# A reordered hand-written schedule around attention: the copies of values, the window sums, and the reload of the residual

## The reference

```python
h = _rmsnorm(x, norm1) @ w_in              # -> c_q (256), c_kv (128), k_rope (32), u (512)
q = einsum('bsr,rhd->bshd', _rmsnorm(c_q, q_a_norm), w_q_b)
kv = einsum('bsr,rhd->bshd', _rmsnorm(c_kv, kv_a_norm), w_kv_b)   # 8 heads, k_nope and v
attn = softmax((q_nope . k_nope + rope(q_rope) . rope(k_rope)) * scale) @ v
pool = einsum('bsgc,gcd->bsgd', window_mean(u) - u, pool_w) * pool_scale  # windows 2, 4, 8, 16
x = x + concat([attn, pool]) @ w_out
up = dwconv3(_rmsnorm(x, norm2) @ w_up); x = x + (silu(gate) * val) @ w_down
x = x + (p @ w_ple_proj) * sigmoid(_rmsnorm(x, norm3) @ w_ple_gate + b_ple_gate)
y = _rmsnorm(x, final_norm)
```

## Time and profile before

| | |
|---|---|
| median of 3 runs | 1244.72 us (1244.24 to 1246.07) |
| the profiled execution | 1244.72 us, span 1242.7 us |
| mean granted TensorE clock | 0.994 |
| TensorE busy | 1204.8 us |
| VectorE, ScalarE, GpSimd busy | 708.8, 462.7, 204.5 us |

### The profile page before, as it was taken

The page is one execution under the profiler, slowest core; times in us unless marked ns, Lnnn a source line. Parts: engine busy times, 40 slices in busy tenths (PEclk is TensorE's granted clock), DMA queues, the critical chain, the costliest instruction groups (busy, mean ns, idle before and its releaser), DMA issues.

```text
span 1242.7 us, 15574 instructions
## 1 busy us (share of the span) xinstructions
PE 1204.8 (97%) x5496; PEld 970.4 (78%) x5496; DVE 708.8 (57%) x979; ACT 462.7 (37%) x744; POOL 204.5 (16%) x216
## 2 busy tenths in 40 slices
PE   6999799999999999999999999999999999999996
PEld 5887666666888888888888888888788888888885
DVE  6648876763577565554555555555433465347665
ACT  5411577774233433323232322323223344325333
POOL 0137532323654000000000000000000021002100
PEclk9999899999999999999999999999999999999999
DMA  5510000104342222232212222221444444443341
GB/s 191 205 43 11 11 12 11 35 18 159 95 119 85 65 90 66 68 102 68 84 61 75 67 68 84 68 84 61 141 135 143 152 143 140 148 126 95 102 145 76
DMA packets 119187, 113.46 MB, mean 91 GB/s; under 512 B 6292, under 2 KB 102891, under 8 KB 118379
## 3 DMA queue, kind: packets, MB, share of 16 engines
q1 hardware_dynamic: 118848, 112.84, 28.8%
q10 hardware_dynamic: 298, 0.11, 0.0%
HBM read 93.01 MB, written 19.92 MB: 91 GB/s over the span
## 4 chain that ended last, share of the span: by engine, by line
PE 90%; DVE 5%; ACT 3%; issue 1%; DMA 1%; POOL 0%; DVEq 0%; SPq 0%; ACTq 0%
PE ps L194 28%; PE ps L196 28%; PE ps L195 28%; PE ps L575 2%; PE ps L556 2%; ACT SF L917 1%; PE ps L450 1%; PE ps L567 1%; DVE WDHL L1330 1%; PE ps L443 1%; DVE TL L1601 1%; DMA WR<-in_w_ple_gate 1%; DVE XL L1191 0%; PE ps L428 0%; DVE XT L1190 0%
## 5 line engine op out<-in xcount | busy, mean ns | idle before, releaser
L194 PE MATMUL ps<-XH,WH 128*128 128x512 f32 x1096 | 434.2, 396 | 8.6 <-DVE XL L1412 5.1
L195 PE MATMUL ps<-XL,WH 128*128 128x512 f32 x1096 | 428.0, 391 | 0.0
L196 PE MATMUL ps<-XH,WL 128*128 128x512 f32 x1096 | 428.0, 390 | 0.0
L229 DVE TENSOR_TENSOR WL<-WR,WH 128x1024 fp32r<-128x1024 f32 (+1 forms) x133 | 175.7, 1321 | 186.9 <-ACT WH L224 186.6
L224 ACT ACTIVATE WH<-WR 128x1024 fp32r<-128x1024 f32 (+1 forms) x133 | 138.1, 1039 | 320.9 <-PE ps L196 310.8
L194 PEld LDWEIGHTS ps<-XH,WH 128*128 128x128 f32 x1096 | 206.4, 188 | 55.4 <-issue 8.8
L195 PEld LDWEIGHTS ps<-XL,WH 128*128 128x128 f32 x1096 | 206.6, 189 | 44.1 <-issue 2.4
L196 PEld LDWEIGHTS ps<-XH,WL 128*128 128x128 f32 x1096 | 206.6, 189 | 43.3
L1063 ACT ACTIVATE SF<-SF,col 128x512 f32<-128x512 f32 x88 | 71.7, 816 | 289.0 <-DVE SF L1475 288.9
L1475 DVE TENSOR_TENSOR SF<-ps,R 128x512 f32<-128x512 f32 x88 | 60.5, 688 | 169.1 <-PE ps L196 163.7
L194 PE MATMUL ps<-GHL,WH 128*128 128x512 f32 x352 | 137.1, 389 | 0.8 <-DVE SF L1475 0.8
(11 more groups left out here) (164 smaller groups left out, 1244.5 us busy)
## 6 DMA issues: line engine op xcount, KB each, us to landing
WR<-in_w_up SPq DMA_DIRECT2D x44, 512.0 KB, 3.8
WR<-in_w_down SPq DMA_DIRECT2D x44, 512.0 KB, 3.6
g_scratch<-SF SPq DMA_DIRECT2D x22, 512.0 KB, 2.8
SF<-g_scratch SPq DMA_DIRECT2D x44, 256.0 KB, 3.7
WR<-in_w_out SPq DMA_DIRECT2D x16, 512.0 KB, 3.7
WR<-in_w_ple_gate SPq DMA_DIRECT2D x16, 512.0 KB, 3.7
WR<-in_w_in SPq DMA_DIRECT2D x8, 512.0 KB, 5.1
xt_scratch<-XT SPq DMA_DIRECT2D x2, 2048.0 KB, 13.0
```

The costliest lines, as they stand in the source:

```text
L194: pe.matmul(out, wh, xh, start=first, stop=False)
L195: pe.matmul(out, wh, xl, start=False, stop=False)
L196: return pe.matmul(out, wl, xh, start=False, stop=last)
L229: dve.tensor_tensor(WL[:, slot(n), base:cols, :], WR[:, slot(n), base:cols, :], WH[:, slot(n), base:cols, :].bitcast(F32), ALU.subtract).t ...
```

## The change

Nothing of the computation differs; only places and waits do.

- SP: the four reload quarters wait once, for `o_lo` 8 (the last output of attention split), instead of `o_ready` 7 for the first two and `o_ready` 8 for the others.
- TensorE: `values(i + 1, 0)` goes from u 8 to u 12 and waits for the row sums of pair i, sequence 0 to be copied; `weigh(i, 0)` no longer waits for the copy of `values(i + 1, 0)`. `project_q(i + 1, 1)` goes from u 11 to u 9.
- ScalarE: in each slot the exponent is ahead of the turned copy; `q_split(i + 1, 1)` from u 13 to 11, the copy of the values from u 9 to 13.
- VectorE: `rotate(i + 1, 1)` from u 12 to 10, `q_low(i + 1, 1)` from 14 to 12. At input tile 7 the window sums of group 1 come behind the splits of the first attention weights instead of ahead of them.

```diff
--- before.py
+++ after.py
@@ -315,9 +315,8 @@
                     for n in range(T_OUT, T_OUT + 4):
                         sp.wait_ge(w_lo, n - 1)
                         sp.dma_start(WR[:, slot(n), :, :], wtile(w["w_out"][:, (n - T_OUT) * P:(n - T_OUT + 1) * P])).then_inc(ring_in[slot(n)], 16)
+                    sp.wait_ge(o_lo, HEADS)
                     for q in range(4):
-                        if q % 2 == 0:
-                            sp.wait_ge(o_ready, HEADS - 1 + q // 2)
                         sp.dma_start(XT[:, q * 2048:(q + 1) * 2048], xt_dram[:, q * 2048:(q + 1) * 2048]).then_inc(xt_back[q], 16)
                 with sp.Fori(0 if s else 2, KT // 2) as i:
                     for c in range(2):
@@ -520,8 +519,8 @@
                 bank = 7 if i else 4 + s
                 if i and s:
                     pe.wait_ge(v_copied, i * 2 + 1)
-                elif i >= 2:
-                    pe.wait_ge(rr_copied, i * 2 - 2)
+                elif i:
+                    pe.wait_ge(rr_copied, i * 2 - 1)
                 for t in range(TT):
                     tok = slice(t * P, (t + 1) * P)
                     o = ps[bank][:, t * P:(t + 1) * P]
@@ -562,7 +561,7 @@
                     pe.wait_ge(dr_ready, i * 2 + s + 1)
                     if i or s:
                         pe.wait_ge(rr_copied, i * 2 + s)
-                    pe.wait_ge(v_copied, i * 2 + s + 1 + (i < HEADS // 2 - 1) * 2)
+                    pe.wait_ge(v_copied, i * 2 + s + 1 + (s and i < HEADS // 2 - 1) * 2)
                     for h in range(2):
                         ins = pe.matmul(ps[7][h * V_DIM:(h + 1) * V_DIM, :], ones[:, 0:V_DIM], DR[h], start=True, stop=True)
                     ins.then_inc(rr_ready, 1)
@@ -614,10 +613,10 @@
                             project_q(i + 1, 0, qf_ready, i * 4 + 4)
                         if u == 7:
                             project_k(i + 1, 0, qf_ready, i * 4 + 5)
-                        if u == 8:
+                        if u == 9:
+                            project_q(i + 1, 1, k_lo, i * 4 + 6)
+                        if u == 12:
                             values(i + 1, 0)
-                        if u == 11:
-                            project_q(i + 1, 1, k_lo, i * 4 + 6)
                         if u == 13:
                             project_q(i + 1, 2, qf_ready, i * 4 + 6)
                         if u == 15:
@@ -938,11 +937,11 @@
 
             def pair(i, last):
                 for u in range(4 * TT):
-                    turned(i, u)
                     if u + 2 < 4 * TT:
                         exponent(i, u + 2)
                     elif not last:
                         exponent(i + 1, u + 2 - 4 * TT)
+                    turned(i, u)
                     if i:
                         if u == 0:
                             k_split(i, 1)
@@ -976,10 +975,10 @@
                             q_split(i + 1, 0)
                         if u == 8:
                             k_split(i + 1, 0)
-                        if u == 9:
+                        if u == 11:
+                            q_split(i + 1, 1)
+                        if u == 13:
                             values(i + 1, 0)
-                        if u == 13:
-                            q_split(i + 1, 1)
                         if u == 15:
                             q_split(i + 1, 2)
                 if last:
@@ -1263,9 +1262,9 @@
                         dve.wait_ge(pads_zero, 1)
                         dve.wait_ge(edge_in, 16)
                     if n == 7:
-                        chained = windows(dve, 1, 0, chained)
                         split_w_lo(dve, T_ATT, T_ATT, cols=4)
                         split_kv_lo(dve, T_ATT + 1, T_ATT + 1)
+                        chained = windows(dve, 1, 0, chained)
                     for s in range(NSEQ):
                         if n > 4:
                             dve.wait_ge(diff_ready[s], n - 4)
@@ -1396,10 +1395,11 @@
                             k_low(i + 1, 0)
                         if u == 9:
                             q_low(i + 1, 0)
+                        if u == 10:
+                            rotate(i + 1, 1)
                         if u == 12:
-                            rotate(i + 1, 1)
+                            q_low(i + 1, 1)
                         if u == 14:
-                            q_low(i + 1, 1)
                             rotate(i + 1, 2)
                 if last:
                     output(i, 0)
```

## The result

The changed kernel took 1256.24 us (1255.38 to 1257.18), the kernel before beside it 1244.52. The ratio is 1.0092, interval [1.0075, 1.0109]: 11.7 us slower, where +9.3 and a range of 1248.2 to 1258.0 were forecast. One number must be known ahead of the rest: the profiled execution of the changed kernel took only 1250.29 us (span 1248.3, mean granted clock 0.994), and its four timed runs had clocks from 0.983 to 0.990. The profile shown first is thus 5.6 us over the one before, about half of what the timed runs show. A second profile of the same kernel, taken as e4, came out at 1256.69 us and shows where one long execution has the rest.

The account below looks back on a forecast made before the run. TensorE, busy 1204.8 of 1242.7 us, was taken to bound the kernel. Values -2.2, pair 0 +1.5, window sums +4.4, reload +3.9 and a clock stretch +1.7 gave +9.3, 1254.0 us, range 1248.2 to 1258.0.

Parts of the forecast that it names:

- The values and the bank: In attention, moving the values removes TensorE's wait for their copy, partly replaced by one for `k_low`: -2.2 us.
- Pair 0: In attention's first pair, exponents ahead of turned copies delay ScalarE and `k_low`, so TensorE stalls: +1.5 us.
- The window sums: Ahead of attention, group-1 sums behind the still waiting weight split delay VectorE and run beside GpSimd: +4.4 us at `mix_low(2)`.
- The reload: Behind attention, late XT quarters delay the residual add and the `w_out` tile 2 split behind it; TensorE waits 3.9 us.
- The stretch at 1.2 GHz behind the stall: In the dense stage behind the reload's wait, one stretch of TensorE at half speed: +1.7 us, lower bound 0.
- Rival (b): Moved sums cost only their plain length, +2.3 us, and no clock stretch follows: +5.5, 1250.2 us; chance 0.22.
- rival (a): Behind attention, the reload is hidden, so its wait and the clock stretch drop out: 1248.4 us; chance 0.06.
- rival (c): Sums and reload both hidden, attention gives its -2.2 and takes 1.5: -0.7, 1244.0 us, no change; chance 0.06.
- Rival (d): Attention's stalls vanish as `k_low` keeps ahead of `project_q(i+1, 1)`: -5.6 us there, 1241.6 us in all; chance 0.05.

Follow-up runs that it names:

- e4: The whole changed kernel once more, unaltered, for a second profile: 1256.69 us for the profiled execution, 1250.37 for the one timed run.
- e5: Kernel before with only `values(i + 1, 0)` moved to u 12 (copy at u 13) and `weigh`'s wait relaxed; `project_q` stays at u 11: 1241.35 us, ratio 0.997.
- e7: As e5, plus `project_q(i + 1, 1)` at u 9 with its rotate and splits moved, exponents in the old order: 1246.27 us, ratio 1.0015 against the kernel before.
- e2: Kernel before with only the group-1 window sums put behind the weight splits: 1249.22 us, ratio 1.0026.
- e11: Kernel before with the reload at `o_lo` 8 and, for sequence 0, VectorE's weight split ahead of the residual add: 1244.78 us, ratio 0.9999.
- e1: Kernel before with only the reload of XT put behind `o_lo` 8: 1251.04 us, ratio 1.0045.
- e8: As e2, plus GpSimd holding its four `diff_low` back until the sums and tile 7 are done: 1248.45 us, ratio 1.0029 against the kernel before.
- e6: As e5, plus the exponent ahead of the turned copy on ScalarE in all pairs: 1239.11 us, ratio 0.9958 against the kernel before.
- e3: Kernel before with only the attention edits: values, relaxed wait, early `project_q`, exponent ahead of turned copy: 1246.68 us, ratio 1.0003.
- e9: As e6, but pair 0 keeps the turned copy ahead of the exponent: 1239.82 us, ratio 0.9948 against the kernel before.

## Why the prediction was right, and where it was not

**The values and the bank.** Forecast -2.2 with the exponents' order in pairs 1 to 3, measured -0.81 - 0.77 - 0.33 = -1.9 by the table. The stall that takes the place of the old one was put at 1.15 us and was 1.01. That the early `project_q` is what eats the gain was argued; e5 and e7 show it (2.0 us a pair). That something is left of the gain is the order's doing: in the old order pairs 1 and 2 are 0.3 us longer than before (e7), and the new order takes 1.08 and 1.03 off them. The prediction missed what lay beside it: with `project_q` left at u 11, moving the values shortens pairs 0 to 2 by 4.75 us.

**Pair 0.** Forecast +1.5, measured +1.36, and the agreement is in part luck. The prediction charged 1.2 us to the exponents' order; on top of the early projection the order costs 0.56 (e7 to the profile after), and the moved values with the early projection make the pair 0.80 longer than before in the old order (e7). The stall for `k_low` was put at 2.7 and was 2.00: `k_low` starts 16.45 us behind the first scores instead of 15.61, 0.8 late and not 1.2, and TensorE comes to it 0.4 us later than was reckoned.

**The window sums.** The mechanism held at every step: the split no earlier (123.80 before, 124.35 after), VectorE idle 3.65 us (forecast 3.8), the sums 6.7 us long (forecast 6.75), the later sums of group 0 alone, 1.9 us long. (The instruction of 0.16 us that the prediction sets beside the multiplication of 1.13 us is a subtraction of the same size; the multiplication itself takes 0.17 us at 142.90 in the profile after, with GpSimd idle, so the reading stands.) The +4.4 was reckoned at `mix_low(2)`, which starts at 144.78 instead of 139.83: +4.95. The prediction then let attention move by as much, with the clock ahead of it as before ("I leave their number alone"), and this is the step that did not hold. From the same start of `mix_low(2)` (144.77 in e4, 144.76 in e2) attention moves by 3.15 in the profile after and by 6.5 and 6.4 in e4 and e2. Before, TensorE had 1.2 GHz for 10.2 us ahead of attention, 3.4 in the earlier trace rows and

```profile
139.40:146.20 6.80, 5.48 (x13) 4.35 (x14) 3.94 (x6) 4.39 (x8) 2.90 (x4) 0.50 0.00 0
```

The profile after has 10.2 us too, but in one piece that ends at 144.0, and full clock where the kernel before still had 1.2 GHz; and attention moves by less than `mix_low(2)` does. In e2 and e4 the piece lasts 17 us and attention moves by more. The idle time of 5.6 us in front of it is twice the longest that TensorE had ahead of attention before. Why it is 10 us in one execution and 17 in another stays open.

**The reload.** Forecast 3.9, measured 3.2. The term that was mis-sized is the split, put at 2.05 us as in the earlier trace rows. It took 1.22 here. That is also its length with GpSimd idle (e11, 306.66), and the 0.8 us went to GpSimd's multiplication instead, 1.83 us against 1.04: in both profiles the one of the two that began first kept its length. The lower bound of 3.1 had allowed for just this. The add itself began 7.6 us after the last attention instruction ended (forecast 7.2). The stretch at 1.2 GHz behind the stall cost 1.7 us in e1 (forecast 1.7), 3.0 in e4 and none in the first profile.

**The sum.** -2.2 + 1.5 + 4.4 + 3.9 + 1.7 = +9.3 stood against -1.9 + 1.4 + 3.15 + 3.0 = +5.6 in one execution and 6.3 us of clock on top in another, +11.9; the median is +11.7. The range held it because it left room for another stretch, so a part of that is luck. Rival (b), sums at their plain length, is out by e2 and e8, though the first profile has just its time (1250.3 against 1250.2), by chance; rival (a) is out by e1, rival (c) by e1 and e2. Rival (d) named -5.6 us for a `k_low` that is always in time. It was not, in this change, yet e6 reached -5.4 by leaving `project_q` at u 11, where TensorE no longer waits for `k_low`.

## What to carry to other kernels

Moving work ahead of something that is not ready gains nothing, and what it displaces lands on the path: look at what the front-runner waits for. In an in-order engine a wait for data that nobody needs yet holds up whatever stands behind it; put the work that others wait for ahead of that wait (e11 took back 5.9 us so). Where two products share a bank, check both bank users after a move, for e7 traded one 1.6 us wait for another of the same length.

## What the runs showed that was not expected

In these runs a stall of TensorE often cost more than its length, and the surcharge varied from one execution to the next: after the 3.2 us stall at the third output tile none (profile after), 1.7 us (e1) or 3.0 us (e4). And the clock did not come back with the work: in e2 TensorE was busy through 139.8 to 151.2 with 40 matmuls at 1.2 GHz, while in the profile after the same work from 144.2 on ran at full clock. Part of that work is in 128-column matmuls for the values; whether that matters was not tried. A granted clock of 0.50 need not cost anything, as from 11 to 25 us in e4, and a recorded 1.00 need not be true, as at the same place in the profile after: the distance from one product to the next (0.43 or 0.23 us for 512 columns) tells the pace. A stretch between 388 and 400 us came in the profiles of e3, e5, e7 and e9 and not in the others. In all four it begins 0.3 us behind 16 products one column wide (L443; in e3 they take 1.84 us from 393.61, and the clock falls at 395.8), with TensorE busy nearly throughout. The kernel before has the same products at 392.55 and e6 at 387.0, and both keep their clock there; what decides between them stays open.
